# Tile addresses at multiples of 512 bytes, and a root-mean-square norm summed with tokens on partitions

## What is computed

```python
def rmsnorm(x, g):
    xf = x.astype(jnp.float32)
    y = xf * lax.rsqrt(jnp.mean(xf * xf, axis=-1, keepdims=True) + EPS)
    return (y * g.astype(jnp.float32)).astype(x.dtype)
...
def modulate_in(x, g, shift, scale):
    return rmsnorm(x, g) * (1 + scale) + shift
```

## Time and profile before

| | |
|---|---|
| three runs | 3038.01, 3047.13, 3048.84 us, median 3047.13 |
| the profiled execution | 3050.23 us, its span 3048.5 us |
| granted TensorE clock, mean of the span | 0.959 |
| busy: TensorE, weight loads, VectorE, ScalarE, GpSimd | 94%, 77%, 56%, 28%, 10% |
| chain that ended last, by engine | TensorE 83%, VectorE 10%, ScalarE 4% |
| HBM read | 252.89 MB, 84 GB/s over the span |

### The profile page before, as it was taken

How to read it: one execution, slowest core, us unless ns; L and a number is a source line. 1 busy time by engine, 2 the same in 40 slices (tenths; PEclk the granted TensorE clock), 3 DMA queues, 4 the chain that set the end, 5 groups by cost and what they waited for, 6 DMA issues and landing times.

```text
span 3048.5 us, 39841 instructions
## 1 busy us (share of the span) xinstructions
PE 2874.7 (94%) x14770; PEld 2340.1 (77%) x14770; DVE 1718.3 (56%) x2840; ACT 856.6 (28%) x1147; POOL 292.2 (10%) x279
## 2 busy tenths in 40 slices
PE   6999999999779999999999899999998979999998
PEld 5888888877543578888888788888876744678887
DVE  7676676669673356766676772222247664443334
ACT  3221122141363332211221422112232264432222
POOL 1000000024322110000000100000004232000000
PEclk8999999999877999999999999999998979999999
DMA  5333333321220013333333232111212220123232
GB/s 201 117 117 124 111 117 139 103 77 55 56 59 7 21 49 117 117 122 107 123 118 117 76 110 70 62 55 63 74 50 84 74 66 7 55 81 101 91 99 84
DMA packets 63374, 264.94 MB, mean 87 GB/s; under 512 B 8880, under 2 KB 11824, under 8 KB 53680
## 3 DMA queue, kind: packets, MB, share of 16 engines
q1 hardware_dynamic: 50608, 180.17, 18.0%
q0 software_dynamic: 11520, 75.11, 7.6%
q10 hardware_dynamic: 1152, 8.39, 0.7%
HBM read 252.89 MB, written 2.10 MB: 84 GB/s over the span
## 4 chain that ended last, share of the span: by engine, by line
PE 83%; DVE 10%; ACT 4%; issue 2%; DMA 1%; POOL 0%; ACTq 0%; SPq 0%; DVEq 0%
PE ps L1431 74%; PE ps L1670 2%; DVE conv_acc L1184 2%; PE ps L1597 2%; PE ps L1625 1%; PE ps L1605 1%; DVE w_lo L934 1%; DVE rstd L987 1%; DVE nmax L1289 1%; ACT e_sb L846 1%; DMA x<-in_xT 1%; ACT probs_t L860 1%; DVE mod_start_acc L1366 1%; DVE y_hi L1023 0%; DVE sq L1011 0%
## 5 line engine op out<-in xcount | busy, mean ns | idle before, releaser
L1431 PE MATMUL ps<-y_hi,w_hi 128*128 128x512 f32 (+1 forms) x3184 | 912.5, 350 | 65.3 <-DVE y_lo L1015 31.2
L1431 PE MATMUL ps<-y_lo,w_hi 128*128 128x512 f32 (+1 forms) x3184 | 907.8, 349 | 0.0
L1431 PE MATMUL ps<-y_hi,w_lo 128*128 128x512 f32 (+1 forms) x3184 | 900.6, 346 | 0.0
L1431 PEld LDWEIGHTS ps<-y_hi,w_hi 128*128 128x128 f32 x3184 | 519.9, 191 | 164.5 <-issue 35.8
L626 ACT ACTIVATE w_hi<-w_raw 128x1024 fp32r<-128x1024 f32 (+1 forms) x290 | 326.6, 1128 | 1063.9 <-PE ps L1431 1063.9
L1431 PEld LDWEIGHTS ps<-y_lo,w_hi 128*128 128x128 f32 x3184 | 517.1, 190 | 75.9
L1431 PEld LDWEIGHTS ps<-y_hi,w_lo 128*128 128x128 f32 x3184 | 515.0, 190 | 77.7 <-issue 0.2
L934 DVE TENSOR_TENSOR w_lo<-w_raw,w_hi 128x1024 fp32r<-128x1024 f32 (+1 forms) x290 | 384.8, 1327 | 322.3 <-ACT w_hi L626 320.0
L949 DVE SCALAR_TENSOR_TENSOR mod_acc<-mod_raw,cact,mod_acc 128x256 f32<-128x256 f32 x896 | 360.2, 479 | 0.0
L1431 PE MATMUL ps<-h_lo,w_hi 128*128 128x512 f32 (+1 forms) x1254 | 356.8, 344 | 0.0
L1431 PE MATMUL ps<-h_hi,w_hi 128*128 128x512 f32 (+1 forms) x1254 | 356.3, 344 | 0.0
(11 more groups left out here) (162 smaller groups left out, 2033.8 us busy)
## 6 DMA issues: line engine op xcount, KB each, us to landing
w_raw<-in_w_up SPq DMA_DIRECT2D x176, 512.0 KB, 3.5
mod_raw<-in_w_mod POOLq DMA_DIRECT2D x64, 1024.0 KB, 5.1
w_raw<-in_w_down SPq DMA_DIRECT2D x64, 704.0 KB, 4.1
w_raw<-in_w_in SPq DMA_DIRECT2D x36, 512.0 KB, 3.5
mod_start<-in_w_mod ACTq DMA_DIRECT2D x8, 1024.0 KB, 22.0
w_raw<-in_w_out SPq DMA_DIRECT2D x16, 512.0 KB, 3.5
stack<-qk_hi SPq DMA_DIRECT2D x48, 96.0 KB, 2.1
band<-in_rpb POOLq DMA_DIRECT2D x16, 224.0 KB, 6.6
```

The costliest lines, as they stand in the source:

```text
L1431: mm = pe.matmul(slot[s][:, at:at + b - a], w[s][:, k, :], r[:, k, a:b], start=(k == 0 and n == 0), stop=(k == kc - 1 and n == 2))
```

## The change

It rounds the base of the tiles up to 512 bytes and orders the small tiles so that x, weights, y, h, act_buf, hid_buf, sq, ssq and the constant matrices all lie at multiples of 512; rstd and the vectors do not. In the norm, each block of 128 tokens of ssq and sq[1] becomes the weights, and one column of ones is moved through it: the sum comes out with tokens on partitions, one column per block. Root and reciprocal then work on 128x4 (128x2 for a half of 256 tokens). `widen_root` brings the result back: for each block the inverse root's column, repeated 128 times, is held as weights and the identity is moved through, which leaves it on all partitions in `turn`. VectorE reads the first half there; GpSimd's product still reads rstd, to which ScalarE copies the second half (`keep_root`). The second half's reciprocal moves from behind chunk 6 to behind chunk 5.

```diff
@@ -70,6 +70,7 @@
 MOD_STEPS = 2 * DC
 MOD_FIRST = 2 * D // MOD_COLS
 QUAD = 32
+LINE = 512
 CONV_LEN = HALO + LAT + HALO + CTX + HALO
...
@@ -217,7 +218,7 @@
     sems = {name: nc.alloc_semaphore(name) for name in SEMAPHORES}
-    cursor = [((nc.sbuf_base + 31) // 32) * 32]
+    cursor = [((nc.sbuf_base + LINE - 1) // LINE) * LINE]
     def place(name, shape, dtype=F32, at=None):
         size = 4 * int(np.prod(shape[1:]))
@@ -235,10 +236,15 @@
     mod_raw = place("mod_raw", [P, DC, MOD_COLS])
     rope_t = place("rope_t", [P, 4, LAT], at=at_mod)
     mod_acc = place("mod_acc", [P, 2, MOD_COLS])
+    ones_r = place("ones_r", [P, P], F32R)
+    ones = ones_r[:, :].bitcast(F32)
+    ident = place("ident", [P, P])
+    pairsum = place("pairsum", [P, P])
+    backward = place("backward", [P, P])
+    quadsum = place("quadsum", [P, P // QUAD, QUAD])
     mod_quads = place("mod_quads", [P, 2 * MOD_COLS // QUAD])
     mod_diag = place("mod_diag", [P, 2 * MOD_COLS // P, P // QUAD])
     mod_out = place("mod_out", [P, 4])
-    quadsum = place("quadsum", [P, P // QUAD, QUAD])
     quad_of = place("quad_of", [P, P // QUAD])
     mod_vec = place("mod_vec", [P, 2, LAYERS * N_MOD * DC])
     mod_bias = place("mod_bias", [P, 1, LAYERS * N_MOD * DC])
@@ -249,27 +255,25 @@
     scale1 = place("scale1", [P, 2, DC])
     gates = place("gates", [P, 2, DC])
     eps_t = place("eps_t", [P, 2])
-    ones_r = place("ones_r", [P, P], F32R)
-    ones = ones_r[:, :].bitcast(F32)
-    ident = place("ident", [P, P])
-    pairsum = place("pairsum", [P, P])
-    backward = place("backward", [P, P])
     mask = place("mask", [P, 2, GRID_W])
     cvecs = place("cvecs", [P, LAYERS, 5, WC])
     ctaps = place("ctaps", [P, LAYERS, WC, CONV_K])
     sub_g = place("sub_g", [P, LAYERS])
     lam_rows = place("lam_rows", [P, LAYERS, 4, DIFF_DH])
     lam = place("lam", [P, 8])
+    std_t = place("std_t", [P, TOK // P])
+    rstd_t = place("rstd_t", [P, TOK // P])
     nmax = place("nmax", [P, 4])
     esum = place("esum", [P, 4])
     rsum = place("rsum", [P, 4])
     nrsum = place("nrsum", [P, 4])
+    at_rstd = cursor[0]
+    rstd = place("rstd", [P, POOL_LEN])
+    cursor[0] = (cursor[0] + LINE - 1) // LINE * LINE
     act_buf = place("act_buf", [P, TOK])
     hid_buf = place("hid_buf", [P, TOK])
     at_sq = cursor[0]
     sq = [place(f"sq{s}", [P, TOK]) for s in range(2)]
-    at_rstd = cursor[0]
-    rstd = place("rstd", [P, POOL_LEN])
     at_ssq = cursor[0]
     ssq = place("ssq", [P, TOK])
     pw_sb = place("pw_sb", [P, WC, W], at=at_ssq)
@@ -582,7 +586,7 @@
                 a, b, _ = halves(tokens)[1]
                 norms[0] += 1
-                pool.wait_ge(sems["rstd"], 2 * norms[0])
+                pool.wait_ge(sems["rstd"], norms[0])
                 for m in range(DC):
                     if m >= 2:
@@ -635,7 +639,15 @@
                 a, b, _ = halves(tokens)[half]
                 t.wait("norm_sum")
-                act.activation(rstd[:, a:b], turn[:, LAT * half:LAT * half + b - a], ACT.Sqrt, bias=eps_t[:, 0:1], scale=1.0 / D).then_inc(sems["norm_sqrt"], 1)
+                act.activation(std_t[:, a // P:b // P], turn[:, LAT * half:LAT * half + (b - a) // P], ACT.Sqrt, bias=eps_t[:, 0:1],
+                               scale=1.0 / D).then_inc(sems["norm_sqrt"], 1)
+
+            def keep_root(tokens):
+
+                a, b, _ = halves(tokens)[1]
+                norms[0] += 1
+                act.wait_ge(sems["rstd_wide"], 2 * norms[0])
+                act.activation(rstd[:, a:b], turn[:, LAT:LAT + b - a], ACT.Copy).then_inc(sems["rstd"], 1)
             def make_y(layer, norm, tokens, after=None):
@@ -661,6 +673,7 @@
             y_made = [0]
             ssq_made = [0]
             hidden = [0]
+            norms = [0]
             for b in range(MOD_FIRST):
                 act.dma_start(mod_start[:, b, :, :], w_mod[b]).then_inc(sems[f"mod_first{b}"], 16)
@@ -677,6 +690,7 @@
             for s in range(2):
                 act.wait_ge(sems[raw_loaded[s]], 16)
                 act.activation(w_hi[s][:, 0:DC, :], raw[s][:, 0:DC, :], ACT.Copy).then_inc(sems["split_hi"], 1)
+            keep_root(TOK)
             make_y(0, 0, TOK)
             def up(p, mods):
@@ -758,6 +772,8 @@
                         split_hi(p, i, 1, p.next_kc)
                     if m == 4:
                         root(p.tokens, 1)
+                    if m == 6:
+                        keep_root(p.tokens)
                 make_y(*norm, p.tokens, after)
                 ssq_made[0] += DC
@@ -984,8 +1000,7 @@
             def invert_root(tokens, half):
                 a, b, _ = halves(tokens)[half]
                 t.wait("norm_sqrt")
-                dve.reciprocal(rstd[:, a:b], rstd[:, a:b]).then_inc(sems["rstd"], 1)
-                t.wait("rstd")
+                dve.reciprocal(rstd_t[:, a // P:b // P], std_t[:, a // P:b // P]).then_inc(sems["norm_inverse"], 1)
             def mods_ready(layer, i):
                 dve.wait_ge(sems["mod_vec"], (mod_chunk(layer, i) + DC) // 2)
@@ -1003,12 +1018,14 @@
                 (a0, b0, _), (a1, b1, _) = halves(tokens)
+                t.wait("rstd_wide")
+                t.skip("rstd_wide")
                 for m in range(DC + 1):
                     if m < DC:
                         if m >= 2:
                             t.wait("affine")
-                        dve.tensor_tensor(sq[m % 2][:, a0:b0], x[:, m, a0:b0], rstd[:, a0:b0], ALU.mult).then_inc(sems["normed0"], 1)
+                        dve.tensor_tensor(sq[m % 2][:, a0:b0], x[:, m, a0:b0], turn[:, 0:b0 - a0], ALU.mult).then_inc(sems["normed0"], 1)
                     if m:
                         t.wait("y_hi")
                         buf = (act_buf, hid_buf)[(m - 1) % 2]
@@ -1156,7 +1173,7 @@
                         add_square(1)
                     if m == 3:
                         split_lo(p, i, 1, p.next_kc)
-                    if m == 6:
+                    if m == 5:
                         invert_root(p.tokens, 1)
                 make_y(p.tokens, after)
@@ -1413,8 +1430,9 @@
             for half, (a, b, _) in enumerate(halves(LAT)):
                 if half:
                     invert_root(LAT, 1)
+                t.wait("rstd_wide")
                 for m in range(DC):
-                    dve.scalar_tensor_tensor(o_final[:, m, a:b], x[:, m, a:b], gain_f[:, m:m + 1], rstd[:, a:b],
+                    dve.scalar_tensor_tensor(o_final[:, m, a:b], x[:, m, a:b], gain_f[:, m:m + 1], turn[:, LAT * half:LAT * half + b - a],
                                              ALU.mult, ALU.mult).then_inc(sems["final"], 1)
@@ -1441,10 +1459,23 @@
                 a, b, _ = halves(tokens)[half]
-                for src, last in ((ssq, False), (sq[1], True)):
-                    pe.wait_ge(sems["square" if last else "sum_squares"], (squares_made if last else ssq_made)[0])
-                    mm = pe.matmul(turn[:, LAT * half:LAT * half + b - a], ones[:, :], src[:, a:b], start=not last, stop=last)
+                pe.wait_ge(sems["sum_squares"], ssq_made[0])
+                pe.wait_ge(sems["square"], squares_made[0])
+                for j in range((b - a) // P):
+                    for src, last in ((ssq, False), (sq[1], True)):
+                        mm = pe.matmul(turn[:, LAT * half + j:LAT * half + j + 1], src[:, a + P * j:a + P * j + P], ones[:, 0:1],
+                                       start=not last, stop=last)
                 mm.then_inc(sems["norm_sum"], 1)
+
+            def widen_root(tokens, half):
+
+                a, b, _ = halves(tokens)[half]
+                t.wait("norm_inverse")
+                for j in range((b - a) // P):
+                    c = a // P + j
+                    mm = pe.matmul(turn[:, LAT * half + P * j:LAT * half + P * j + P], rstd_t[:, c:c + 1].to_broadcast([P, P]),
+                                   ident[:, :], start=True, stop=True)
+                mm.then_inc(sems["rstd_wide"], 1)
             def run_last(p, b0, with_mod, rhs_hi, rhs_lo):
@@ -1465,6 +1496,8 @@
                             ssq_made[0] += DC - 1
                             squares_made[0] += DC
                             norm_reduce(p.tokens, 0)
+                        if s == 0 and k == p.kc // 3 + 4:
+                            widen_root(p.tokens, 0)
                         mm = product(s, k, p.kc, rhs_hi, rhs_lo, [(a1, c1, LAT)])
                     mm.then_inc(sems["unit_done"], 1)
                 ssq_made[0] += 1
@@ -1489,6 +1522,8 @@
                             for step in range(LAG[half] + p.kc):
                                 if half == 0 and step == 3 and pair0:
                                     norm_reduce(p.tokens, 1)
+                                if half == 0 and step == 6 and pair0:
+                                    widen_root(p.tokens, 1)
                                 for s, k in ((0, step), (1, step - LAG[half])):
                                     if 0 <= k < p.kc:
```

(5 more changed lines are left out.)

## The result

| | before | after |
|---|---|---|
| median of 14 runs each | 3046.9 us (3032.6 to 3061.9) | 3061.7 us (3052.9 to 3066.3) |
| ratio, with 95% interval | | 1.0054 (1.0037 to 1.0072) |
| profiled execution, its span | 3050.2, 3048.5 us | 3056.7, 3055.1 us |

The account below looks back on a forecast made before the run. TensorE, busy 94% of the span, was taken as the bound, set by the pace of one matmul. Start -1.0, norms +4.0, end +0.4 and addresses nothing gave 3.4 us gained: 3043.7 us forecast, range 2990 to 3075.

Parts of the forecast that it names:

- The start: Start of the kernel: TensorE at the low clock replaces VectorE as the bound, and 1.0 us is lost.
- The five norms: Norms between phases: shorter root and reciprocal and an earlier second half gain 4.0 us, bounds 0 and 8.
- rival 3: At the norms, one-column work drops the clock, up to 1.7 us before w_hi, five times: 8 us, 3052; chance 0.08.
- The effect I feared: First half of each norm: 0.9 us of wideners push ScalarE's split w_hi back, so little of the gain is kept.
- The new wait: Second half of each norm: ScalarE's copy, ahead of chunk 7's affine, waits about 1.3 us for TensorE's wideners.
- The end: Final norm: shorter reciprocal, but the inverse root must pass TensorE (0.5 us and a wait); 0.4 us gained.
- The addresses: Every matmul: moving tiles to multiples of 512 bytes costs nothing; named the widest unknown.
- rival 1: All products: address moves remove the 13 ns excess, 2874, half 2960, or the slower second pace, 3026; chance 0.36.
- rival 2: Steady products: weights and y at one residue collide, each product pays, 45 us, 3092; chance 0.14.
- the side that I gave 0.14: Whole kernel: the chance that the change makes it slower, against 0.36 faster and 0.50 the same.
- The two rules of the Trainium skill: GpSimd reading SBUF blocks two-SBUF-input VectorE instructions; back-to-back matmuls take N/2.4 GHz plus about 2.5 ns.
- the hope that most of the 13 ns could be had: All products: by the skill's matmul rule, 11 of the 13 ns over the columns would be avoidable.

Follow-up runs that it names:

- both mends: Changed kernel with 128 columns of ones through each block and the second half's wideners at step 5; median 3031.8 us, ratio 0.9946.
- addr_only: Kernel before with only the constant LINE, the rounding and the order of the tiles changed, old norm kept; ratio 1.0009.
- both_even: Kernel of both mends, up-phase pairs moved as 384 and 384 columns instead of 512 and 256, except the first behind a norm; median 3014.7 us, ratio 0.9884.
- ones_wide: Changed kernel with 128 columns of ones moved through each block instead of one (the tables' "128 columns"); ratio 1.0011.

## Why the prediction was wrong

**The start: right in one execution of two.** I gave TensorE 132 instructions x 0.2135 = 28.2 us from 28.95, the bound in VectorE's place, and a loss of 1.0. The second execution of the kernel after:

```profile
28.91 5.25 PE ps L1466 x24
34.16 13.65 PE ps L1732 x64
47.82 2.77 PE ps L1476 x12
50.59 6.63 PE ps L1742 x32
```

They sum to 28.3 us; the first product of the first phase comes at 60.88 instead of 59.80, 1.1 later. In its first execution the last 32 ran at the high clock (3.52 us) and the start gained 2.0, inside the two ends I gave (a loss of 1.0, a gain of 4.8). In the four other traces with the one-column reduce the first product came twice at 58.0 and twice at 61.0 or 61.1: the row I took is one of two outcomes, not the expected one.

**The five norms: the step that failed.** I summed 4.0 us gained, with bounds of 0 and 8; the traces show 8.2 and 13.0 lost. The instructions' own lengths were right, reduce and reciprocal (164 ns) included. What failed was the clock at which TensorE does them, and with it the wait for TensorE in front of ScalarE's copy. I priced reduce, products and wideners at the high clock because all rows of the norms before were so, and kept the low clock for one sentence in rival 3. Per norm, in us after the reduce's start, for the norm behind the first down phase, from the timelines:

| | before | after, 2nd execution | 128 columns | both mends |
|---|---|---|---|---|
| y_lo of chunk 0 done | 9.6 | 10.9 | 9.3 | 9.3 |
| ScalarE's copy starts | none | 24.0 | 21.1 | 19.6 |
| y_lo of chunk 7 done | 23.6 | 26.5 | 23.6 | 22.2 |
| last y_lo done | 32.3 | 35.2 | 32.3 | 30.9 |

With the high clock (third column) y_lo of chunk 0 comes 0.2 us sooner than before (9.33 against 9.55); I had said 0.35 behind a down phase. The effect I feared, w_hi pushed back by the wideners, is there: it ends at 6.9 instead of 6.0, 0.9 later as said. But the sum of 4.0 was too large even so. With 128 columns the five norms are 0.4 us longer than before: four of them save 1.0 in all, nearly all of it at 1110 us, where I had 3.5, and the one at 2264 us, with its low stretch, loses 1.4. So of what the norms missed, 12.2 and 17.0 us in the two executions, 4.4 are gains that I counted and that 128 columns do not bring either, and 7.8 and 12.6 go with the one-column reduce.

**The new wait: placed right at the high clock, undersized at the low one.** I had the copy wait 1.3 us, behind six products of 1.4 us that follow y_lo of chunk 5. With 128 columns, so at the high clock, it waits 1.5, and at the norm of 1110 us y_lo of chunk 7 is done 22.4 us after the reduce's start, my figure (1133.2 less 1110.8), against 23.6 before; behind a down phase it is level, where I had 0.5 gained. In the kernel after it waits 2.97: TensorE was still busy with step 4 when y_lo of chunk 5 came, and twelve products, most of their time at 1.2 GHz, stood ahead of the wideners. That the wait could be had for nothing, by one step earlier, I did not see: y_lo of chunk 7 then comes 1.4 us sooner than before the change.

**The end.** I gave 0.4 gained. From the final norm's first reduce to the end the kernel before takes 22.1 us in its second execution and the kernel after 21.9: 0.2 gained. The widening of the second half, which I gave 0.5 us and a wait, took 1.24.

**The addresses: right in the sum, wrong in the reason.** Nothing was the cost I took, and addr_only measures 1.0009 (0.9987 to 1.0030). But a row does react: the steady pairs changed by 1.9%. Neither rival 1 (every product faster) nor rival 2 (every product slower, 3092) is what happened: the same two paces as before occur, in another order. Which one the old addresses get is drawn; the new ones get both in turn. In rival 1 I wrote that the second pace "is explained by nothing in the loops"; it was drawn, and a second trace of the same kernel would have said so.

**Rival 3 had the mechanism.** "The low clock spreads", up to 1.7 us in front of w_hi at each norm, 8 us, 3052, at a chance of 0.08. w_hi ended 2.5 us later than before where 0.9 was the wideners', so 1.6 was the clock's: the size was right for the first half. The second half, which costs as much again, was missing. The measured median, 3061.7, is inside my range but on the side that I gave 0.14.

**The two rules of the Trainium skill.** The y_lo of chunk 6 took 0.69 us at 643.05 instead of 1.21, with GpSimd's normalising not yet begun. By the rule in "SBUF — State Buffer" (Who interferes with whom) of the Trainium skill that is as it should be, and the trace agrees. "TensorE: Matmul & The Clock Gate" (Part 1) of the Trainium skill has back-to-back matmuls at N/2.4 GHz plus about 2.5 ns. The fp32r products here never came below 13 ns over the columns: two products of 384 columns take 0.347 us even in both_even (320 for the columns), so the measurement decides against the hope that most of the 13 ns could be had.

**Still open.** What draws the pace at a phase's start; why the address of one small operand lets it turn over; what draws the mixer's clock. The traces of the kernel after are 8.2 and 13.0 us longer in the norms, the medians differ by 14.9 us; how much of the rest is the mixer's and the pace's draw was not measured, as only one execution of each set is traced. Nor is it known why the one-column reduce lets the clock fall at some norms and not at others (two of five in the first execution, four of five in the second), and what brings the later low stretches, which the kernel before has as well.

## What to carry to other kernels

Trading a long VectorE instruction for many one-column matmuls is safe only if TensorE's clock holds behind them: look at what the next dozen products take, and if they run at half speed, move as many columns as cost nothing. A broadcast back through TensorE puts its queue between two other engines; place it where its operand is ready and TensorE would wait anyway, not one step later. And trace the old kernel twice before reading a pace from it: here one trace could not tell a property of the program from a draw.

## What the runs showed of the hardware

- One column or 128 through the same kind of block costs TensorE the same (1.92 and 2.02 us for 16 instructions), but behind the one-column reduce the granted clock fell to 1.2 GHz, 1.6 to 3.2 us from its start, in four of the five norms of the kernel after's second execution; with 128 columns it stayed at 2.4 GHz for at least 18 us behind the reduce's start in all five norms of ones_wide (and at least 13.6 us in the three other traces with 128 columns).
- The same 96 products have two paces in one program, 0.31 us apart, which is 20 ns for each of the 16 steps of k. Most of them are spent in one of the step's three pairs of products: by the starts in the traces 361 ns to the next start, where the other two take 349 and 350 (all three take 347 at the short pace). The lines below show it in the kernel after, in a long pair of units. In the kernel before's second execution it is the same one, y_lo with w_hi, from 80 to 250 us. Products of 384 columns alone never did this, nor those of 512 alone: a down phase behind 2700 us lasted 59.84 us in every trace.

```profile
117.08 0.53 PE L1449 MATMUL ps<-y_hi,w_lo 128*128 128x512 f32 x2
117.44 0.51 PE L1449 MATMUL ps<-y_lo,w_hi 128*128 128x512 f32 x2
117.79 0.51 PE L1449 MATMUL ps<-y_hi,w_hi 128*128 128x512 f32 x2
118.14 0.53 PE L1449 MATMUL ps<-y_hi,w_lo 128*128 128x512 f32 x2
```

- The clock column can be wrong at the start of a trace: the second execution of the kernel after shows 1.00 over a window in which instructions come every 0.2 us, the pace of the 0.50 window in the earlier trace rows. The first record of a change of clock stands only at 65.9 us there. The pace of known instructions is the safer reading.

```profile
34.10:41.00 6.90, 6.90 (x34) 6.90 (x34) 6.90 (x21) 2.38 (x3) 0.00 (x0) 1.00 0.49 167
```
